# One in six low weight parts of the merge loop moves from GpSimd to VectorE

## The reference

```python
ys = jnp.stack([y_a, y_b, y_c], axis=2)
branch = jnp.einsum('bsnc,ncd->bsnd', ys, w_branch[layer])
gates = jax.nn.sigmoid(p_gate.reshape(bsz, seq, N_BRANCH, D_MODEL))
merged = jnp.sum(gates * branch, axis=2)
h = h + merged @ w_o[layer]
```

## Time and profile before

| | |
|---|---|
| median of 3 runs | 2012.46 us (2009.29 to 2016.42) |
| span of the profiled execution, first to last instruction | 2010.0 us |
| PE busy | 1878.0 us, 93% of the span |
| DVE busy | 1288.2 us, 64% |
| ACT busy | 1093.3 us, 54% |
| POOL busy | 916.6 us, 46% |
| mean granted clock of PE | 0.962 of full speed |

### The profile page before, as it was taken

One profiled execution on the slowest core, in us unless ns is written; L12 is line 12 of the kernel. 1 busy time (PEld: TensorE's weight loads), 2 busy tenths in 40 slices (PEclk: granted clock), 3 DMA queues, 4 the chain that ended last, 5 costly groups with the idle time before them and its releaser, 6 DMA issues.

```text
span 2010.0 us, 43300 instructions
## 1 busy us (share of the span) xinstructions
PE 1878.0 (93%) x15850; PEld 1747.4 (87%) x15850; DVE 1288.2 (64%) x1956; ACT 1093.3 (54%) x1862; POOL 916.6 (46%) x662
## 2 busy tenths in 40 slices
PE   9898889999999898889999989998899999989999
PEld 8878778999999878778999988866899997669999
DVE  4587725679924487825679963576786536777754
ACT  5653455557755643455557755665555547465543
POOL 4543449929986543449919985721100024220000
PEclk9999889999999999989999999997999999879999
DMA  6432015656665432005656655420466653215665
GB/s 213 134 111 66 11 38 158 178 159 184 188 182 175 140 109 72 23 30 153 176 159 182 186 164 156 143 89 21 135 185 200 186 168 108 76 31 166 188 187 165
DMA packets 146916, 271.12 MB, mean 135 GB/s; under 512 B 16433, under 2 KB 16946, under 8 KB 146738
## 3 DMA queue, kind: packets, MB, share of 16 engines
q1 hardware_dynamic: 145296, 264.97, 44.5%
q10 hardware_dynamic: 1442, 3.66, 0.5%
HBM read 267.52 MB, written 1.05 MB: 134 GB/s over the span
## 4 chain that ended last, share of the span: by engine, by line
PE 57%; DVE 21%; POOL 11%; ACT 8%; issue 3%; DMA 0%; ACTq 0%; DVEq 0%; SPq 0%
PE bank L668 56%; POOL ring_split L1360 11%; ACT arena L1394 6%; DVE arena L2468 4%; DVE hidden_lo L1949 3%; DVE hidden_hi L1948 2%; DVE arena L2474 2%; PE bank L810 1%; ACT hi_ring L1394 1%; DVE u_split L2035 1%; DVE u L2030 1%; DVE arena L2558 0%; DVE arena L2190 0%; DVE small L2284 0%; DVE arena L2282 0%
## 5 line engine op out<-in xcount | busy, mean ns | idle before, releaser
L1360 POOL TENSOR_TENSOR ring_split<-ring,hi_ring 128x512 fp32r<-128x512 f32 x602 | 847.7, 1436 | 798.4 <-ACT hi_ring L1394 795.1
L1394 ACT ACTIVATE hi_ring<-ring 128x512 fp32r<-128x512 f32 x890 | 549.6, 630 | 524.1 <-PE bank L668 479.5
L668 PE MATMUL bank<-u_hi,hi_ring 128*128 128x256 f32 (+1 forms) x2160 | 617.9, 286 | 31.4 <-POOL ring_split L1360 30.6
L668 PE MATMUL bank<-u_split,hi_ring 128*128 128x256 f32 (+1 forms) x2160 | 605.5, 280 | 0.0
L668 PE MATMUL bank<-u_hi,ring_split 128*128 128x256 f32 (+1 forms) x2160 | 605.4, 280 | 0.0
L668 PEld LDWEIGHTS bank<-u_hi,hi_ring 128*128 128x128 f32 (+1 forms) x2160 | 404.7, 187 | 44.2 <-POOL ring_split L1360 31.5
L668 PEld LDWEIGHTS bank<-u_split,hi_ring 128*128 128x128 f32 (+1 forms) x2160 | 404.5, 187 | 1.7
L668 PEld LDWEIGHTS bank<-u_hi,ring_split 128*128 128x128 f32 (+1 forms) x2160 | 405.1, 188 | 1.0
L2074 DVE TENSOR_TENSOR ring_split<-ring,hi_ring 128x512 fp32r<-128x512 f32 x288 | 194.1, 695 | 114.1 <-ACT hi_ring L1394 111.0
L668 PE MATMUL bank<-hidden_hi,hi_ring 128*128 128x256 f32 x864 | 244.7, 283 | 13.4 <-POOL ring_split L1360 13.3
L668 PEld LDWEIGHTS bank<-arena 64*64 64x64 f32 (+3 forms) x3680 | 211.8, 156 | 50.9 <-issue 31.2
(11 more groups left out here) (265 smaller groups left out, 2502.3 us busy)
## 6 DMA issues: line engine op xcount, KB each, us to landing
ring<-in_stream SPq DMA_DIRECT2D x1002, 256.0 KB, 2.6
par<-in_params ACTq DMA_DIRECT2D x3, 637.0 KB, 3.9
h<-in_x SPq DMA_DIRECT2D x4, 256.0 KB, 4.0
cst<-in_cst SPq DMA_DIRECT2D x1, 993.0 KB
out<-h ACTq DMA_DIRECT2D x3, 256.0 KB, 2.7
par<-in_params ACTq DMA_DIRECT2D x1, 633.0 KB, 6.5
out<-h ACTq DMA_DIRECT2D x2, 128.0 KB, 2.2
msk<-in_masks SPq DMA_DIRECT2D x1, 104.0 KB
```

The costliest lines, as they stand in the source:

```text
L668: ins = nc.tensor.matmul(o, l, r, start=start, stop=stop)
L1360: G.tensor_tensor(ring_lo[:, c, :], ring[:, c, :], hi_ring[:, s % HI_RING, :].bitcast(F32), ALU.subtract).then_inc(lo_by_pool, 1)
L1394: return nc.scalar.activation(o, i, f, **kw)
```

## The change

Every sixth piece of the merge loop's names, counted from the start of the layer (number 5 modulo 6), becomes VectorE's; the other five stay GpSimd's. VectorE gets one more `lo.upto` ahead of the loop.

```diff
+SHARED1, SHARE = {n for m in MERGE for n in m[:2]}, 6
...
-    def add(self, sizes, by_vector, whole):
+    def add(self, sizes, by_vector, whole, shared=()):
...
-                maker = "whole" if name in whole else "vector" if name in by_vector else "pool"
+                mine = name in by_vector or name in shared and (len(self.maker) - first) % SHARE == SHARE - 1
+                maker = "whole" if name in whole else "vector" if mine else "pool"
...
-                owners.add(*((SIZES2, BY_VECTOR2, WHOLE2) if kind == SECOND else (SIZES1, BY_VECTOR1, WHOLE1)))
+                owners.add(*((SIZES2, BY_VECTOR2, WHOLE2) if kind == SECOND else (SIZES1, BY_VECTOR1, WHOLE1, SHARED1)))
...
                 split(C, yc, yc_hi, yc_lo, S["yc_split"])
 
+                lo.upto(MERGE[0][0], 0)
                 for g in range(2):
                     B.wait(dve, f"GM{g}")
```

## The result

The changed kernel takes 2037.9 us (median of 4 runs, 2033.15 to 2038.16) against 2012.56 before: ratio 1.0126, 95% interval 1.0102 to 1.015, so 25 us slower (20 to 30). Forecast were 20.8 us and 2033. The profiled execution ran 2037.93 us with a span of 2036.1.

What follows compares the result with a forecast made beforehand. GpSimd's late low parts were taken to hold both merge loops above TensorE's pace. Stalls of 2 x 13.3, less 9.0 of lateness, plus 3.2 for the clock gave +20.8 us, so 2033 us; range 2007 to 2058 us.

Steps and rivals of the forecast that it cites:

- What goes, 9.0 us: Both merge loops, steps 1 to 9: all of GpSimd's lateness goes, 4.8 and 4.2 us, 9.0 us in all.
- The place in the order: Merge loop: VectorE makes piece 95+6i behind all its work of step i; lone durations give stalls of 3.1 us a layer.
- Holds, 13.3 us of stalls a layer: Merge loop: VectorE's instructions ahead of the low part wait 0.98 us per GpSimd hold; TensorE stalls 13.3 us a layer.
- t0: Merge loop: moment when TensorE goes on after `M` of step i; it needs piece 95+6i 4.24 us later.
- the upper end: Merge loop: every listed VectorE instruction waits its 0.98 us, giving stalls of 36 us a layer.
- The clock: TensorE's granted clock falls behind step 6's stall of 4.55 us, adding 1.6 us a layer, 3.2 us in all.
- The sum: Whole kernel: 2 x 13.3 - 9.0 + 3.2 = +20.8 us, so 2033 us.
- The rule of the port: GpSimd locks the shared port for its whole instruction: each hold 0.32 us more, 3.7 us a layer, sum about 2040 us.

## Why the prediction was right

- **What goes, 9.0 us: right.** After the change no window of steps 1 to 9 waits for GpSimd, and where the new wait is avoided the kernel gains 7 to 9 us against before (ratios 0.9959 and 0.9954 of 2010.61 us are 8.2 and 9.2; their windows of steps 1 to 8 give back 6.9 and 7.0 of the 9.0 us). At the loop's start little went, as said: 11.59 and 11.78 us after against 11.16 and 11.99.
- **The place in the order: right.** The stall is ahead of the last gate piece, released by VectorE, in each step but 7; the two runs that change the place or the piece alone remove it.
- **Holds, 13.3 us of stalls a layer: nearly right, by errors that partly cancel.** Counted were 11.5 holds, there were 13; by the ends below the stalls are 14.9 us. The ends of the low parts were forecast at t0 plus 5.4, 5.65, 5.3, 6.5, 5.5, 8.7 in steps 1 to 6 and 4.67 in steps 8 and 9. Measured after, by the same rule as in step 6 above: 5.97, 6.75, 5.29, 6.36, 6.61, 7.70, 4.69, 4.69. Step 1 met two holds, where I took 1.5; steps 2 and 5 met one more than I counted. In step 2 the two gatings of 128x256 take 1.01 us alone, not 0.87 (I had the 0.42 from another instruction, and so took a hold of 1.00 us from their 1.42 where 0.92 is right), so that VectorE's cast ended 0.1 us past GpSimd's first request, and the hold came ahead of the next instruction instead of behind it. Step 6 met two, not three, holds: GpSimd's third instruction started only at 380.28, waiting 3.06 us for a high part. The count `pieces_used` of a piece rides on TensorE's next matmul (line 673 of the kernel before), which is the one that stalls, so the third high part can't come before the stall ends. That is read from code and timeline, not tried by itself. The terms of the upper end, a bound that nothing came near, are off by up to 0.13 us each: with 0.98 us a hold they sum to 36.3 us, not 35.8.
- **The clock: its price right (1.53 against 1.6 us), its count luck.** The ground for it was that step 6's stall would be longer than the idle time of 3.92 us in the earlier trace rows; TensorE was idle for 3.29 us, and the clock fell all the same. The kernel before already showed a fall behind less: 0.85 in the window from step 0 to 1, 0.54 in its first 3.6 us, behind an idle time of 2.02 us. In the profiled execution it fell at step 6 only, as forecast; in the variants' profiles it fell at steps 2, 4 or 5 as well, where I had counted nothing.
- **The sum.** The windows of steps 1 to 8 grew by 22.4 us, with step 9's stalls 23.5 us, where I had 20.8. The medians' 25.3 us include that in their interval.
- **The rule of the port.** By the whole-instruction form of it (the Trainium skill, SBUF — State Buffer, "SBUF: two separate sides") each hold would be 1.30 us. The traces stay with about 0.98: 1.67 us for a low part of 0.69, 2.20 for 1.23. A memset of GpSimd, which reads nothing, held VectorE up in no instruction of the loop. For VectorE's instructions with two SBUF inputs this agrees with the words of the same section that the GpSimd instruction has to read SBUF to be in their way: a low part that began at 352.16, 0.03 us behind a fill, took 0.69 us. No cast of VectorE began during a fill in the first loop, so for casts these runs show nothing of it.

## What to carry to other kernels

Work given to a faster engine is only as early as its place in that engine's queue: before sharing pieces out, list for each one when its consumer needs it and what stands ahead of it, and give the engine the piece whose input and deadline fit the moment at which it is free. Here the same share cost 25 us with one remainder of the division by six and gained 9 us with another. Two engines that hold each other up by turns have longer instructions than the lone ones, and such a list must be made with both.

## What the runs showed of the hardware that I had not expected

- TensorE's granted clock fell behind an idle time of 2.33 us in one execution (window at 0.86) and not behind the same 2.33 us in another (1.00), with the same instructions around it. Which of the two happens is open.
- GpSimd's memset of 128x512 takes 0.53 us against 1.30 for the subtraction, and beside it VectorE keeps its lone durations. Two fills of the first loop took longer, 0.76 us from 323.87 and 0.62 us from 350.71; each began while a cast or a scaling of VectorE was running (323.47 to 324.16, 350.00 to 350.87) and ended 0.46 to 0.47 us behind its end.
- Eight plain float32 matmuls of 256 columns with 128x128 weights show as 16 records and take 3.62 us, 0.45 us each; filling an idle time with them kept the clock at 1.00.
